# Softmax denominators in four 32-column tiles, spread by DMA, and an own norm chain for q from step 9, in a hybrid attention and gMLP layer

## The reference, cut to what matters

```python
h = rms_norm(x, norm_g) * (1 + scale) + shift            # (S=2048, D=1024) per sequence
z = h @ w_in                                             # 8704 columns
for g, (window, dilation) in enumerate(((128, 1), (512, 4), (2048, 16))):
    q = partial_rope(rms_norm(z_q[g], q_norm_g[g]), positions)   # 8 heads x 64
    k = partial_rope(rms_norm(z_k[g], k_norm_g[g]), positions)
    o[g], lse[g] = dilated_window_attention(q, k, z_v[g], window, dilation)
attn = sum_g softmax_g(lse)[g] * o[g]      # = sum_g numerator_g / sum_g denominator_g
y_a  = attn * silu(z_gateA)
u, v = gelu(z_uv); v = layer_norm(v)
y_b  = u * (causal W_s @ v + b_s) * silu(z_gateB)
merged = sigmoid(z_mA) * (y_a @ w_branch_a) + sigmoid(z_mB) * (y_b @ w_branch_b)
out  = x + gate * (merged @ w_out)
```

## Time and profile before

| | |
|---|---|
| median of 3 runs | 733.54 us (732.09 to 735.17) |
| profiled execution, own time | 731.77 us |
| its span on the slowest core (core 6) | 730.1 us |
| spans of all cores | 726.2 to 730.1 us |
| mean granted clock of TensorE on the cores | 0.988 to 0.993 |
| PE busy | 708.1 us, 97% of the span |
| DVE, ACT, POOL busy | 64%, 50%, 41% of the span |

### The profile page before, as it was taken

One profiled execution on the slowest core, in us unless ns is written; L12 is line 12 of the kernel. 1 busy time (PEld: TensorE's weight loads), 2 busy tenths in 40 slices (PEclk: granted clock), 3 DMA queues, 4 the chain that ended last, 5 costly groups with the idle time before them and its releaser, 6 DMA issues.

```text
span 730.1 us, 14355 instructions; the slowest of 8 cores (726.2 to 730.1 us)
## 1 busy us (share of the span) xinstructions
PE 708.1 (97%) x4651; PEld 357.3 (49%) x4651; DVE 465.0 (64%) x781; ACT 363.1 (50%) x690; POOL 301.3 (41%) x386
## 2 busy tenths in 40 slices
PE   8788999999999999999999999999999999999997
PEld 3444455445666665555554444444444444444443
DVE  6547898875598888888888864556753232333234
ACT  3746878878655555566666555565221111111110
POOL 1805243452545565533334003577342343433435
PEclk9889999999999999999999999999999999999999
DMA  8996135674466686621312608039980222322234
GB/s 249 327 183 170 35 97 112 83 111 60 59 88 96 93 88 76 91 53 26 28 37 30 102 1 138 7 60 181 186 235 33 71 104 68 106 59 57 61 114 173
DMA packets 71257, 72.07 MB, mean 99 GB/s; under 512 B 48656, under 2 KB 55184, under 8 KB 70928
## 3 DMA queue, kind: packets, MB, share of 16 engines
q0 software_dynamic: 18528, 25.43, 23.9%
q1 hardware_dynamic: 50208, 37.47, 21.7%
q10 hardware_dynamic: 2448, 8.26, 2.8%
HBM read 74.82 MB, written 8.39 MB: 114 GB/s over the span
## 4 chain that ended last, share of the span: by engine, by line
PE 81%; DMA 5%; DVE 4%; ACT 4%; issue 3%; POOL 1%; SPq 1%; DVEq 0%; ACTq 0%; POOLq 0%
PE ps L238 71%; DVE arena L247 4%; ACT arena L247 4%; DMA arena<-w_ada 4%; PE ps L658 3%; PE ps L694 2%; PE ps L543 2%; PE ps L699 2%; DMA arena<-arena 1%; POOL arena L247 1%; SPq L250 1%; PE ps L1059 0%; PE ps L356 0%; PE ps L616 0%; SPq L277 0%
## 5 line engine op out<-in xcount | busy, mean ns | idle before, releaser
L238 PE MATMUL ps<-arena 128*128 128x512 bf16 x2604 | 578.5, 379 | 4.6 <-DVE arena L247 4.1
L247 POOL TENSOR_TENSOR arena<-arena 128x128 bf16<-128x128 f32 (+5 forms) x308 | 259.0, 849 | 374.6 <-DVE arena L247 300.6
L238 PEld LDWEIGHTS ps<-arena 128*128 128x128 bf16 x2604 | 271.5, 107 | 284.0 <-issue 19.8
L247 ACT ACTIVATE arena<-ps 128x1024 bf16<-128x1024 f32 (+2 forms) x283 | 191.7, 708 | 251.1 <-PE ps L238 156.5
L247 DVE TENSOR_TENSOR arena<-ps,arena 128x512 bf16<-128x512 f32 (+2 forms) x215 | 166.4, 794 | 62.0 <-PE ps L238 24.4
L247 ACT ACTIVATE arena<-arena 128x8 f32<-128x8 f32 (+8 forms) x272 | 114.4, 432 | 74.4 <-DVE arena L247 46.7
L247 DVE SCALAR_TENSOR_TENSOR arena<-arena,ps 128x512 f32<-128x512 f32 x80 | 54.6, 687 | 110.1 <-PE ps L238 91.9
L247 DVE TENSOR_TENSOR arena<-arena 128x1024 bf16<-128x1024 bf16 (+5 forms) x112 | 78.7, 706 | 22.9 <-POOL arena L247 10.7
L247 DVE TENSOR_REDUCE arena<-arena 128x8 f32<-128x512 bf16 x96 | 65.0, 681 | 30.4 <-ACT arena L247 29.8
L247 DVE SCALAR_TENSOR_TENSOR arena<-arena 128x512 f32<-128x512 f32 (+3 forms) x40 | 31.8, 796 | 10.2 <-DMA arena<-w_adag 5.0
L247 DVE TENSOR_SCALAR arena<-arena 128x512 bf16<-128x512 bf16 (+5 forms) x57 | 27.2, 477 | 12.8 <-DMA arena<-w_ada 5.6
(11 more groups left out here) (44 smaller groups left out, 172.8 us busy)
## 6 DMA issues: line engine op xcount, KB each, us to landing
arena<-x SPq DMA_DIRECT2D x30, 512.0 KB, 4.9
arena<-w_in POOLq DMA_DIRECT2D x44, 256.0 KB, 5.1
out<-arena ACTq DMA_DIRECT2D x15, 512.0 KB, 5.2
arena<-w_ada SPq DMA_DIRECT2D x12, 512.0 KB, 12.8
arena<-w_in POOLq DMA_DIRECT2D x6, 1024.0 KB, 13.8
arena<-w_adag SPq DMA_DIRECT2D x8, 512.0 KB, 8.1
arena<-w_out POOLq DMA_DIRECT2D x2, 1024.0 KB, 22.7
arena<-w_ada POOLq DMA_DIRECT2D x3, 512.0 KB, 8.5
```

The costliest lines, as they stand in the source:

```text
L238: ins = e.matmul(out_ap, l, r, start=(i == 0), stop=(i == n - 1))
L247: P.op(eng, lambda e: getattr(e, meth)(*a, **kw), reads=reads, writes=writes)
```

## The change

The denominators move to four column tiles of 32: each of the four weights blocks is `ones64[:, 0:32]`, tile `j` holds head half `j % 2` of head group `j // 2`, and all four write one bank (`PB[1]`, 256 columns), while `PB[0]` takes the numerators of all heads (512 columns). `accum(s, 0)` now moves 512 columns of numerators and `accum(s, 1)` 256 columns of denominators. In `acc` a denominator stands on 32 rows only, with both pairs of its tile side by side; `spread(tb)` copies it, for 512 tokens, to the 64 rows of its head with eight DMAs on the SP queue, and the multiplication by the denominators is taken out of `finA` as `finC`, which waits for them. Spreads are issued at the end of turns 39, 43 and 47 and after `accum(47, 1)`. The loads of the first two weights of branch B wait for spreads 2 and 3.

Besides, q gets its own `rstd` and an early `scaleqk` from turn 9 on instead of 16; `kgain` moves behind `pv` in turns below 18; in turns 10 to 13 one of the two weight loads moves ahead of `rope`; in the prologue `phase(2, 0, (0, 1))` moves ahead of `proj(4, 0)`, `rstd(4, 0, 8)` and `scaleqk(4, 0)` move back, and `x_sq(6)` moves into turn 4.

```diff
 def pv(s):
-            o = [banks[PB[h]].rearrange("p (n a q) -> p n a q", n=2, a=2) for h in range(2)]
+            num = banks[PB[0]].rearrange("p (m q) -> p m q", m=4)
+            den = banks[PB[1]][:, 0:256].rearrange("p (a q) -> p a q", a=2)
...
-                for h in range(2):
-                    for ki_ in range(nk):
-                        for e_ in range(2):
-                            ins = e.matmul(o[h][64 * e_:64 * e_ + 64, 1, :, :], ones64, pp[h][:, e_, :, ki_, :],
+                for ki_ in range(nk):
+                    for j in range(4):
+                        ins = e.matmul(den[32 * j:32 * j + 32], ones64[:, 0:32], pp[j // 2][:, j % 2, :, ki_, :],
+        def spread(tb):
+            ts_ = slice(tb * 512, (tb + 1) * 512)
+            for j in range(4):
+                for x_ in range(2):
+                    r0 = 64 * (j % 2) + 32 * x_
+                    P.op("sp", lambda e, j=j, r0=r0: e.dma_start(
+                        out=accv[r0:r0 + 32, 6 + tb % 2, 1024 * (j // 2):1024 * (j // 2) + 1024].rearrange("p (a q) -> p a q", a=2),
+                        in_=accv[32 * j:32 * j + 32, 4:6, ts_]),
+                        reads=["acc1_%d" % tb], writes=["db%d_%d" % (tb % 2, 2 * j + x_)], slot="db%d" % (tb % 2))
+        def finC(hp, tb):
+            X("dve", "scalar_tensor_tensor", [k1] + ["db%d_%d" % (tb % 2, j) for j in range(8)], [k1], out=f1, in0=f1, scalar=1.0,
+              in1=accv[:, 6 + tb % 2, 512 * hp:512 * hp + 512], op0=ALU.add, op1=ALU.mult)
 last(1), s == 3:
+                    phase(2, 0, (0, 1))
                     proj(4, 0)
...
+        QS = 9
...
-            if it >= 16:
+            if it >= QS:
                 rstd(it, 0, 8)
...
-            kgain(it - 2)
+            if it >= 18:
+                kgain(it - 2)
...
-            if it >= 16:
+            if it >= QS:
                 scaleqk(it, 0)
...
             pv(c_)
+            if it < 18:
+                kgain(it - 2)
...
-            rope(it)
+            for n in (0, 1):
+                if n:
+                    rope(it)
+                if 10 <= it < 14:
+                    n += 2 * (it - 10)
+                    load_w(4 + n // 4, 3584 + 512 * (n // 4), n % 4, n % 4 + 1)
...
+            if it in (39, 43, 47):
+                spread((it - 39) // 4)
...
-                load_w(0, OFF_Z_B)
-                load_w(1, OFF_GATE_B)
+                load_w(0, OFF_Z_B, gate=["db0_%d" % j for j in range(8)])
...
+        accum(47, 1)
+        spread(3)
+        load_w(1, OFF_GATE_B, gate=["db1_%d" % j for j in range(8)])
```

More of the change, by code:

```diff
@@ L701, in fn, with accum @@
                 return ins
             P.op("pe", fn, reads=ptk(pt_of[(s, 0)]) + ptk(pt_of[(s, 1)]) + ["vr%d" % (k_ % NV) for k_ in kb], writes=[B(PB[0]), B(PB[1])])
-        def accum(s, h):
+        def accum(s, d):
             g, blk = steps[s]
-            dst, o = acc[:, h, :, tok_slice(g, blk)], banks[PB[h]].rearrange("p (m q) -> p m q", m=4)
-            if g == 0 and (h == 1 or s > 4):
-                X("act", "copy", [B(PB[h])], ["acc%d" % h], out=dst, in_=o)
+            ts_ = tok_slice(g, blk)
+            dst = accv[:, 4:6, ts_] if d else accv[:, 0:4, ts_]
+            o = banks[PB[d]][:, 0:256 if d else 512].rearrange("p (m q) -> p m q", q=128)
+            ks = ["acc%d_%d" % (d, n) for n in ((blk // 4,) if g == 0 else range(4) if g == 2 else (blk % 4,))]
+            if g == 0 and (d == 0 or s > 4):
+                X("act", "copy", [B(PB[d])], ks, out=dst, in_=o)
@@ L750, in V1 @@
             mm_group(banks[b], [(hT[:, kc, t * 128:(t + 1) * 128], wslot[3][:, kc, :]) for kc in range(KC)], reads=wk(3), writes=[B(b)])
-            rd = [B(b)] + ["ya%d_1" % hp for hp in range(4)]
+            rd = [B(b)] + ["ya%d_%d" % (hp, 1 if t < 12 else 3) for hp in range(4)]
             if t % 2:
@@ L833, in build_nc @@
         sumsq(4, 0)
-        phase(2, 0, range(3))
-        phase(2, 1, range(3))
+        phase(2, 1, (0, 1))
+        phase(2, 0, (2,))
+        phase(2, 1, (2,))
         sc_own(5)
         x_load(9)
-        rstd(4, 0, 8)
-        scaleqk(4, 0)
         phase(2, 2, range(3))
@@ L842, in build_nc @@
         transp(1, (1,), 4)
+        rstd(4, 0, 8)
         for s in range(3):
@@ L845, in build_nc @@
             vevac(s, "act" if s == 1 else "dve")
+        scaleqk(4, 0)
         x_transp(5, TB)
@@ L895, in build_nc @@
                 rstd(it, 8, 16)
-                accum(c_, 0)
+                accum(c_, 1)
             if it - 1 in fin_at:
+                finC(*fin_at[it - 1])
                 finB(*fin_at[it - 1])
@@ L943, in build_nc @@
         mask(45, 1)
+        finC(0, 2)
         finB(0, 2)
         finZ(1, 2)
+        scores(46, 0)
         accum(44, 0)
         accum(44, 1)
+        mask(46, 0)
         transp(47)
         V1(1)
-        scores(46, 0)
-        mask(46, 0)
         finA(1, 2)
+        finC(1, 2)
         V1(2)
@@ L964, in build_nc @@
         finA(2, 2)
+        finC(2, 2)
         V1(4)
@@ L975, in build_nc @@
         finA(3, 2)
+        finC(3, 2)
         pv(47)
@@ L991, in build_nc @@
         finA(2, 3)
+        finC(2, 3)
         finB(1, 3)
@@ L994, in build_nc @@
         finA(3, 3)
+        finC(3, 3)
         finB(2, 3)
```

43 lines of the change are left out of this document (21 added, 22 removed).

## The result

The changed kernel takes 727.25 us (median of four runs, 726.90 to 727.37), the kernel before took 733.14 on the same chip (four runs, 732.09 to 735.17): a ratio of 0.9916, 95% interval 0.9893 to 0.9938. The forecast was 7.5 less. Times and ratios leave out executions in which one die took over 1% longer than the other at a lower granted clock. In the last stage chips differ by some 3 us (from pv 47 to the end 316.3 to 317.1 us on one die of e0_after, 313.7 to 313.8 on the other), so totals of different chips are compared only through their ratios.

What follows compares the result with a forecast made beforehand. The prediction took PE's busy time and its waits to bound the kernel. Denominators 3.2, q's norm chain 2.5 and prologue 1.8 us summed to 7.5, taking 733.5 to 726.0 us, with a range of 719.5 to 731.0.

Steps and rivals of the forecast that it cites:

- main case: Whole kernel: all three gains arrive and the tile-shape change costs 4.8 us; 726.0 us, own range 723.5 to 728.5, chance 0.55.
- Denominators, 3.2 us: In pv: four tiles at once save 8.0 us, 48 added changes of tile shape cost 4.8, leaving 3.2.
- no cost for 64 to 32 columns: Rival, in pv: switching from numerator to denominator tiles is free; 721.2 us, chance 0.20.
- four tiles run no faster: Rival, denominators: four tiles only match two pairs, so the shape change is paid for nothing; 734.0 us, chance 0.08.
- the round of 0.135 us: Denominators: in-between estimate from a skill page for a four-tile round; saving 5.9 us, time 728.1.
- q's norm chain, 2.5 us: Turns 9 to 15: scaling q before k's reduction removes q projection waits for DVE; 2.5 us, between nothing and 3.4.
- The discount for ACT: Turns 9 to 15: 2.5 us taken instead of 3.4, as added work would put ACT over 90% busy.
- the 3.4: Turns 9 to 15: PE's waits, all of the q projection for DVE, 3.4 us; the upper end of that gain.
- The slower rival: Turns 12 to 15: late kgain delays k's scaling on ACT and PE pays; 737 us or more, chance 0.05.
- Prologue, 1.8 us: Prologue: moved matmuls, norm steps and square remove PE waits of 0.50, 0.94 and 0.68 us; 1.8 us, lower end nothing.
- the waits only move: Rival, turns 9 to 15 and prologue: only 0.5 of 4.3 us remains; 729.8 us, chance 0.12.
- Edits costed at nothing: Lighter accum, spread, finC and gated weight loads: taken as 0 us, PE being covered by over 2 us at finC.

Runs made afterwards that it cites:

- e0_after: The changed kernel measured again, unaltered, on another chip: ratio 0.9939 to the kernel before.
- e8: The changed kernel with the numerators in 32-column tiles too: 729.44 us, where the kernel before took 732.15.
- e1: The kernel before with only the order edits (prologue, q's own norm chain, late kgain, moved loads): ratio 0.9962 to the kernel before.
- e2: The changed kernel with all order edits undone, leaving four-tile denominators, spread and finC: ratio 0.9993 to the kernel before.
- e6: The changed kernel with kgain back at its early place in all turns: ratio 0.9944 to the kernel before.
- e5: The changed kernel with q's own norm chain only from turn 16, kgain still late: ratio 1.0017 to the kernel before.
- e3: The changed kernel without the spread, finC reading acc directly (wrong rows for most heads): ratio 0.9925 to the kernel before.
- e10: The changed kernel with kgain behind pv in all turns, also from 18 on: ratio 0.9936 to the kernel before.
- e4: The changed kernel with the weight load of turns 17 to 28 also moved ahead of rope: ratio 0.9948 to the kernel before.

## Why the prediction was right, and where its sum was off

The time of 727.25 lies in the main case's own range, and 1.25 above its value. The stages let each term of the sum be read against the runs.

*Denominators, 3.2 us.* Right in both parts and in the difference. A round of four takes as long as a pair did: e8, with two rounds, has 165.60 - 165.28 = 0.32 us from its first denominator to the projection, which is what two pairs had the earlier trace rows. The change from 64 to 32 columns costs 0.10 us. This decides three cases at once: "no cost for 64 to 32 columns" and "four tiles run no faster" fall, and so does the round of 0.135 us that stood between. The Trainium skill's rule (TensorEngine Tiling (Array Packing), Tiling Modes, Key Properties) that a change of tiling mode drains the engine agrees with the 0.10 us here; its 2.38 for three column tiles (TensorE: Matmul & The Clock Gate, Part 3) was not measured as such, but four tiles here gave the whole factor of two over two tiles. In the loop the term is 0.40 + 0.75 + 0.50 us (pv 12 to 20, 36 to 43, and 43 to 47 with the spread away) and, once q's wait is gone, 1.17 + 0.11 more (pv 5 to 12 and 0 to 5, the changed kernel against e1): 2.9 in all. That this is near 3.2 is partly luck. Of the 1.17 some 0.7 are seven steps at 0.10; the rest are waits that got shorter in the three steps from pv 7 to 10 (they gain 0.18, 0.28 and 0.28 us on core 0 instead of 0.10). In pv 0 to 5, where q still waits in turns 6 and 8, four steps with two key blocks give 0.11 instead of 0.4. What the prediction didn't say is that this holds only together with q's chain; alone, e2 shows 0.5 us for the whole half.

*q's norm chain, 2.5 us.* The cause is right, the size by luck: 2.40 by e1. Nearly all waits of the q projection are gone, which was the upper end: turns 9 to 15, 55.85 us in the earlier trace rows, take 52.7 in e1 on cores 0 and 6, and the prediction had 52.4 without a wait. The discount for ACT wasn't needed: its share came out at 45.10 / 51.57 = 87%, not over 90%, and PE shows no new wait for ACT at the k projection. But the 3.4 was read on one core, 6, with 55.48 us between pv 5 and 12, where the median core has 54.75 and so less to lose. The slower rival, kgain in front of k's scaling, didn't come: with q's own chain kgain's place costs nothing (e6), as forecast. Without that chain the late kgain and the moved loads together lose 1.8 us (e5); which of the two does was not tried.

*Prologue, 1.8 us.* Mis-sized: about 0.6. The three waits were named rightly and two are gone, but the lower end, nothing, that the prediction gave ("if the same engines are late one instruction further on") is nearer the truth than its value, only that the late engine is POOL: 0.54 and 0.77 us at the transposes of q and k. PE's waits between 57 and 80 us were to be under 1 us; they are 2.1 to 3.3 by core, where the core of the earlier trace rows had 3.2. Here the rival "the waits only move" was right.

*Edits costed at nothing.* One of them costs. The spread costs 0.5 us (e3). The issue price was taken from a row of another shape: 0.59 us for a copy of 32 partitions within SBUF against 0.33 for a tile of 128 from memory, so that eight issues end 2.6 us later. DVE's wait at finC was to stay below a microsecond, and is 0.61, 1.28 and 3.39; the cover that was named, the next q projection and scores, took most of it. Another loss was not on the list at all: through DVE's waits for transposes pv 20 to 36 grew, by 0.15 us in the median on one chip and 0.64 on the other, by 2.5 on the slowest core of the profile. That kgain is what waits and that its place in DVE's list decides is shown by e10. From issue to landing the transposes of this stretch hardly changed in the median (4.4 to 4.7 us by core before, 4.5 to 5.0 after); single ones land late: the longest takes 7.4 to 7.7 us on the four cores where PE waits 0.6 us or more at pv, 6.2 to 6.7 on the others, 6.0 to 6.6 before. e10 has them up to 7.9 us, and PE doesn't wait. Why single ones land later is not shown: they are the same transposes in the same turns, e4 speaks against the loads' order, and since e1 and e2 have the waits as well, no single part of the change is needed for them. Steps 20 to 35 have one key block, so PE isn't quicker there either. The cause stays open; as only one execution of the kernel before was profiled, that it waits as long on other chips isn't excluded.

Put together: 2.9 + 2.4 + 0.6 - 0.5 - (0.15 to 0.64) = 4.8 to 5.3 us, and the median core's span fell by 727.85 - 722.62 = 5.2; from pv 47 to the end, which the sum leaves out, the median fell by 0.3 (313.65 to 313.39). Against the forecast of 7.5 that leaves out 1.2 us at the prologue, 0.5 at the spread, 0.3 at the denominators and the rest at kgain.

## What to carry to other kernels

Savings on one engine don't add up edit by edit: where PE waits for DVE in a turn, a shorter PE stage is waited away until the wait itself is taken out, so the two edits belong together and are to be priced together. Count the changes of tile shape as well as the streaming: 0.10 us each took half of the gain from four tiles in steps with two key blocks, and all of it in steps with one. Price a DMA issue by a row of the same shape, and put an instruction that waits for a DMA as far down its engine's list as its reader allows, since all that stands behind it waits too; then look at what it delays there, for in pv 36 to 43 the same move cost 0.6 us. And read a wait on more than one core before pricing it: between pv 5 and 12 the cores of one execution differed by 2.3 us.

## What the runs showed of the hardware

Thirty-two matmuls of 128 columns with their own 32-column weights took 0.46 us, 14 ns each, no longer than sixteen with 64 columns (0.47), so neither issue nor weight loading limited four tiles at this size. A copy of 32 partitions within SBUF took 0.59 us of SP's queue, more than the 0.33 of a 512 KB tile, and landed 2.4 us after its issue (2.3 to 3.0). DMA transposes landed 2.4 to 7.7 us after theirs, with a median of 4.3.
